# The last norm of a transformer trunk, moved from a stage of its own into the expert loop

## The chip, the cores and the metric

The kernel runs on one core of a Trainium2 chip. The metric is the device time of one execution in microseconds (us). Engines are named as in the profile: PE is TensorE, PEld its weight loads, DVE is VectorE, ACT is ScalarE, POOL is GpSimd, SP is SyncE (here it only issues DMAs). All data is float32.

## The reference, cut to what matters

One layer of a trunk over 2048 tokens of width 1024: token mixing, cross-attention to a memory, then a mixture of 32 experts, and a norm over the result. The change touches only the last two:

```python
def rmsnorm(x, g):
    y = x * rsqrt(mean(x * x, axis=-1) + EPS)
    return y * g

# group top-1, then the top 2 of its 8 experts: every token visits two experts
x = x + sum over the token's two experts e of gate * ((silu(h @ w1[e]) * (h @ w3[e])) @ w2[e])
return rmsnorm(x, norm_final)
```

## The kernel before, in words

The visits (two for each token, 4096 in all) are sorted by expert and padded to blocks of 128 slots for each expert. 47 blocks are in use in this run. route (from line 1849) works out for every slot its token (slot_rows, a row number; an empty slot has a number past the end, 4096, and an indirect DMA skips it) and its gate (slot_gates). hm_scratch holds the normed inputs of all tokens, x_scratch (x2 in the code) the residual stream in DRAM.

run_experts (line 2051) goes through the blocks, one "turn" for each. Each engine has its own written-out order, and they meet at semaphores:

- TensorE, step(b): the products with w1 and w3 into g_ps and u_ps, the transposes of the next block's inputs (xg), the product with w2 of the block before into y_ps, the transposes of h. Each product is made of three, of parts cut high and low (split_product).
- ScalarE, step(b): cuts the high parts of the next expert's w13 weights (high_w13, line 1830), silu, the high part of x, then scales y_ps by the gates into exp_y (line 2215), which waits for y_free, then the high part of h and of w2 (line 2224).
- DVE, step(b): the low parts of the same (lines 1834, 2262, 2238, 2258), 12 operations of 128x1024 in a block that is the first of its expert, and silu times u.
- POOL, in a turn: gather(b + 3) brings the inputs of a later block from hm_scratch into xg (line 1845), after TensorE's transposes of the block before it; scatter(b) waits that the scatter before has landed, raises y_free, waits for ScalarE's scaling (y_scaled), copies the slot's rows (line 2156) and adds exp_y to x_scratch by an indirect DMA with an add (line 2159).
- SP loads the weights: next_w13 for expert e when the products of expert e - 2 are done, next_w2 likewise.

When the last scatter has landed, POOL raises all_stored, and SP loads the first tiles of x_scratch and the gains over the weights (FinishLoads). finish_norm (line 2326) then runs over 16 tiles of 128 tokens: load (SP), square with a sum (ScalarE, line 2362), mean (DVE, line 2374), power of -1/2 (POOL, line 2350), scaling by that and by the gains (DVE, line 2378), store (ScalarE's queue).

## Time and profile before

| | us |
|---|---|
| median of 3 runs | 2643.79 (2642.81 to 2645.5) |
| the profiled execution | 2644.87 |
| its span in the trace | 2643.1 |
| TensorE busy | 2515.5 (95%) |
| DVE, ScalarE, POOL busy | 1477.4, 1284.2, 603.5 |
| last scatter starts | 2590.84 |

Times in the rows are us from the start of the span, unless marked ns. A group of instructions shows how many there were (x47), their busy time, the mean ns of one, and what the engine had waited for ahead of them. POOL's DMA_INDIRECT is the generation of descriptors; the transfer itself goes on after it, up to its landing.

### The profile page before, as it was taken

To read this page: it belongs to the slowest core of one execution; us is meant where nothing else is said; L and a number is where in the kernel's file an instruction comes from. 1 tells how busy PE (TensorE), PEld (TensorE's weight loads), DVE (VectorE), ACT (ScalarE), POOL (GpSimd) and SP (SyncE) were. 2 spreads that over 40 slices of the span, in tenths; PEclk is the share of its full clock that TensorE was granted. 3 is DMA by queue.
4 is the path that set the end of the run, shared out by engine and by line. 5 is a ranking of instruction groups with operands and counts; after the bars stand their busy time and mean duration, and the time that the engine had idled before them with its cause. 6 is when DMAs were issued, how large, how long until landed. Compare 5 with 4: busy or idle time off the path is not lost. (4 is left out here: it accounts for less than half of the span.)

```text
span 2643.1 us, 44806 instructions
## 1 busy us (share of the span) xinstructions
PE 2515.5 (95%) x14538; PEld 2053.4 (78%) x14539; DVE 1477.4 (56%) x1943; ACT 1284.2 (49%) x2286; POOL 603.5 (23%) x650
## 2 busy tenths in 40 slices
PE   9999999999999999989999999799999999999991
PEld 7888888676666678886888888678877888888880
DVE  5221343698888864444333333666988755565653
ACT  5221211698898941133222222346878654565643
POOL 0000011477777720000000000012212222112223
PEclk9999999999999999999999999799999999999996
DMA  7433231314201033233121221448999866586757
GB/s 264 165 124 125 84 150 42 100 34 148 73 18 45 2 120 120 96 148 108 62 89 71 92 74 66 170 147 303 388 376 372 295 208 202 197 293 209 264 162 273
DMA packets 141439, 414.83 MB, mean 157 GB/s; under 512 B 22016, under 2 KB 30720, under 8 KB 140288
## 3 DMA queue, kind: packets, MB, share of 16 engines
q1 hardware_dynamic: 125040, 371.15, 38.0%
q0 software_dynamic: 13968, 33.59, 5.4%
q10 hardware_dynamic: 2304, 8.39, 0.8%
q8 instruction: 81, 1.33, 0.2%
q14 instruction: 46, 0.38, 0.0%
HBM read 338.60 MB, written 91.75 MB: 163 GB/s over the span
## 5 line engine op out<-in xcount | busy, mean ns | idle before, releaser
L685 POOL TENSOR_TENSOR stick_weight<-stick_weight,stick_left 128x512 f32<-128x512 f32 (+3 forms) x320 | 327.9, 1038 | 126.5 <-DVE stick_left L817 121.9
L1834 DVE TENSOR_TENSOR moe_w_lo<-moe_w_lo_raw,moe_w_hi (+1 forms) x256 | 298.6, 1219 | 61.9 <-ACT moe_w_hi L1830 32.2
L1830 ACT CAST moe_w_hi<-moe_w_lo_raw (+1 forms) x256 | 256.3, 1053 | 51.5 <-DMA moe_w_lo_raw<-in_w 25.6
L817 DVE TENSOR_TENSOR_SCAN stick_left<-stick_z_ps,stick_left,stick_any_row 128x512 f32<-128x512 f32 x192 | 240.1, 1274 | 35.4 <-ACT stick_z_ps L780 35.1
L778 ACT ACTIVATE stick_weight<-stick_z_ps 128x512 f32<-128x512 f32 (+3 forms) x320 | 173.7, 543 | 32.7 <-PE stick_z_ps L727 21.0
L740 PE MATMUL stick_t_ps<-all_ident,stick_weight 128*128 128x128 f32 x1088 | 165.3, 281 | 18.9 <-ACT stick_weight_t L787 9.1
L780 ACT ACTIVATE stick_z_ps<-stick_z_ps 128x512 f32<-128x512 f32 (+3 forms) x320 | 165.7, 518 | 10.2
L740 PEld LDWEIGHTS stick_t_ps<-all_ident,stick_weight 128*128 128x128 f32 x1088 | 116.0, 141 | 69.8 <-issue 46.1
L75 PE MATMUL exp_g_ps<-moe_w_hi,exp_x_hi 128*128 x376 | 151.8, 404 | 11.5 <-DVE exp_x_lo L2238 11.5
L1845 POOL DMA_INDIRECT moe_xg<-hm_scratch,moe_now x50 | 68.0, 1361 | 405.1 <-PE exp_x_ps L2274 268.0
L75 PE MATMUL proj_z_ps<-proj_w_hi,proj_h_hi 128*128 128x512 f32 x384 | 152.1, 396 | 2.5 <-DVE proj_h_lo L403 2.5
L2262 DVE TENSOR_TENSOR moe_w_lo<-moe_w_lo_raw,moe_w_hi 128x1024 f32 (+1 forms) x128 | 148.1, 1216 | 8.7 <-ACT moe_w_hi L2224 8.3
L75 PE MATMUL exp_y_ps<-moe_w_hi,exp_h_hi 128*128 128x512 f32 x376 | 150.4, 400 | 2.3 <-DVE exp_h_lo L2258 2.3
L76 PE MATMUL proj_z_ps<-proj_w_lo,proj_h_hi 128*128 128x512 f32 x384 | 150.2, 391 | 0.0
L77 PE MATMUL proj_z_ps<-proj_w_hi,proj_h_lo 128*128 128x512 f32 x384 | 150.1, 391 | 0.0
L77 PE MATMUL exp_g_ps<-moe_w_hi,exp_x_lo 128*128 x376 | 147.5, 392 | 0.0
L76 PE MATMUL exp_g_ps<-moe_w_lo,exp_x_hi 128*128 x376 | 147.0, 391 | 0.0
L77 PE MATMUL exp_y_ps<-moe_w_hi,exp_h_lo 128*128 128x512 f32 x376 | 147.0, 391 | 0.0
L76 PE MATMUL exp_y_ps<-moe_w_lo,exp_h_hi 128*128 x376 | 146.7, 390 | 0.0
L77 PE MATMUL exp_u_ps<-moe_w_hi,exp_x_lo 128*128 x376 | 146.6, 390 | 0.0
L75 PE MATMUL exp_u_ps<-moe_w_hi,exp_x_hi 128*128 x376 | 146.3, 389 | 0.0
L76 PE MATMUL exp_u_ps<-moe_w_lo,exp_x_hi 128*128 x376 | 146.3, 389 | 0.0
(291 smaller groups left out, 5811.4 us busy)
## 6 DMA issues: line engine op xcount, KB each, us to landing
moe_w_lo_raw<-in_w SPq DMA_DIRECT2D x384, 512.0 KB, 12.3
proj_w_lo_raw<-in_w_in SPq DMA_DIRECT2D x40, 256.0 KB, 6.3
proj_xs<-in_x SPq DMA_DIRECT2D x16, 512.0 KB, 4.5
qt_scratch<-proj_qk_out SPq DMA_DIRECT2D x16, 512.0 KB, 2.8
kt_scratch<-proj_qk_out SPq DMA_DIRECT2D x16, 512.0 KB, 2.7
mix_q<-qt_scratch SPq DMA_DIRECT2D x16, 512.0 KB
mix_out_xs<-in_x SPq DMA_DIRECT2D x16, 512.0 KB, 4.4
x_scratch<-mix_out_xs SPq DMA_DIRECT2D x16, 512.0 KB, 3.0
```

The source lines that it names most:

```text
L75: pe.matmul(out, left_hi, right_hi, start=first, stop=False)
L76: pe.matmul(out, left_hi, right_lo, start=False, stop=False)
L77: return pe.matmul(out, left_lo, right_hi, start=False, stop=last)
L685: nc.gpsimd.tensor_tensor(taken, taken, after, ALU.mult).then_inc(weight_done, 1)
L740: last = nc.tensor.transpose(t_ps[:, n % 2, b], weight[:, n % W_SLOTS, b * P:(b + 1) * P], ident)
L778: nc.scalar.activation(weight[:, n % W_SLOTS, 0:keys], z, ACT.Sigmoid).then_inc(take_done, 1)
L780: nc.scalar.activation(z, z, ACT.Sigmoid, scale=-1.0).then_inc(leave_done, 1)
L817: nc.vector.tensor_tensor_scan(row[:, c * BANK:c * BANK + keys][:, ::-1], back, any_row[:, 0:keys], start, ALU.mult, ALU.bypass).then_inc( ...
L1830: nc.scalar.copy(self.w13_hi[:, self.w13_at(e, i)], self.w13_raw[:, self.w13_at(e, i)]).then_inc(self.w13_cut, 1)
L1834: ops.tensor_tensor(self.w13_lo[:, self.w13_at(e, i)], self.w13_raw[:, self.w13_at(e, i)], as_f32(self.w13_hi[:, self.w13_at(e, i)]), ALU. ...
L1845: nc.gpsimd.indirect_dma_start(out=self.xg[:], out_offset=None, in_=self.hm, in_offset=bass.IndirectOffsetOnAxis(ap=self.now[:].bitcast(U3 ...
L2262: nc.vector.tensor_tensor(w2_lo[:, w2_at(e, i)], w2_raw[:, w2_at(e, i)], as_f32(w2_hi[:, i]), ALU.subtract).then_inc(w2_ready, 1)
```

## The change

There is no last stage. A token's last visit is the one in the later block. route marks it (is_last) and adds 2048 to the row number of that slot. So slot_rows tells three kinds of slots apart: below 2048 (first visit), 2048 to 4095 (last visit), 4096 (empty).

- scatter(b) adds exp_y to x_scratch for first visits only; the others are out of bounds and skipped.
- ask(b) brings the residual rows of a block's last visits from x_scratch into a new tile end_sb; it is issued at the end of the turn before. list_ends makes the row numbers for it in four small operations.
- finish(b) adds exp_y to end_sb on POOL, ScalarE squares end_sb with a sum, POOL multiplies end_sb by the gains into exp_y once the scatter has landed, makes mean plus EPS and its power, scales exp_y by it, and writes exp_y to the output rows by an indirect DMA. y_free is raised when that DMA (out_stored) has landed. A row whose sum is not complete or a slot that is empty is skipped.
- gather makes its row numbers with two more small operations.
- The silu is written into exp_h instead of a tile of its own, to make room; DVE multiplies in place. ScalarE's silu then waits for the transposes of h. The square's unused output lies over exp_h.
- The gains are loaded by SP within the expert loop, and POOL waits for them ahead of scatter(0).
- FinishLoads and finish_norm are gone.

```diff
     def gather(self, nc, pool, b, slot_rows, xt_done):
         wait_past(pool, self.gathered, 16 * b)
-        nc.gpsimd.tensor_copy(self.now[:], slot_rows[:, bass.ds(b, 1)]).then_inc(self.listed, 1)
+        tokens = self.hm.shape[0]
+        nc.gpsimd.tensor_copy(self.now[:, 7:8], slot_rows[:, bass.ds(b, 1)]).then_inc(self.copied, 1)
+        pool.wait_ge(self.copied, b + 1)
+        pool.sem_inc(self.list_seen, 1)
+        nc.gpsimd.tensor_scalar(self.now[:, 4:5], self.now[:, 7:8], tokens, tokens, ALU.is_ge, ALU.mult).then_inc(self.halved, 1)
+        pool.wait_ge(self.halved, b + 1)
+        pool.sem_inc(self.list_seen, 1)
+        nc.gpsimd.tensor_tensor(self.now[:, 0:1], self.now[:, 7:8], self.now[:, 4:5], ALU.subtract).then_inc(self.listed, 1)
...
+                for k in range(2):
+                    link(nc.vector.tensor_tensor(is_last[:, k], dest[:, k], dest[:, 1 - k], ALU.is_gt))
+                link(nc.vector.scalar_tensor_tensor(out=token_end[:], in0=is_last[:], scalar=float(tiles * P),
+                                                    in1=token[:].unsqueeze(1).broadcast_to([P, 2, tiles]), op0=ALU.mult, op1=ALU.add))
...
                 next_w2(1, True)
+                sp.dma_start(gains[:], gain_out.partition_broadcast(P)).then_inc(gains_loaded, 16)
                 with sp.Fori(3, experts) as e:
                     next_w13(e)
                     next_w2(e - 1, False)
                 next_w2(experts - 1, False)
-                sp.wait_ge(all_stored, 1)
...
                 def scatter(b):
                     if not isinstance(b, int):
-                        pool.wait_ge(stored, 16 * b)
+                        pool.wait_ge(out_stored, 16 * b)
                         pool.sem_inc(y_free, 1)
                     pool.wait_ge(y_scaled, b + LEAD + 1)
...
+                def finish(b):
+                    if isinstance(b, int):
+                        pool.wait_ge(end_cleared, 1)
+                        list_ends(b)
+                        pool.wait_ge(ask_listed, 1)
+                    else:
+                        pool.wait_ge(asked, 16 * b)
+                    nc.gpsimd.tensor_tensor(end_sb[:], end_sb[:], y_sb[:], ALU.add).then_inc(added, 1)
+                    nc.gpsimd.tensor_copy(end_now, ask_now).then_inc(end_listed, 1)
+                    pool.wait_ge(added, b + 1)
+                    pool.sem_inc(end_seen, 1)
+                    pool.wait_ge(stored, 16 * (b + 1))
+                    nc.gpsimd.tensor_tensor(y_sb[:], end_sb[:], gains[:], ALU.mult).then_inc(weighed, 1)
+                    pool.wait_ge(squared, b + LEAD + 1)
+                    pool.sem_inc(end_seen, 1)
+                    nc.gpsimd.tensor_scalar(half[:, 2:3], half[:, 1:2], EPS, None, ALU.add).then_inc(meaned, 1)
+                    pool.wait_ge(meaned, b + 1)
+                    nc.gpsimd.tensor_tensor(half[:, 3:4], half[:, 2:3], half[:, 0:1], ALU.pow).then_inc(rooted, 1)
+                    pool.wait_ge(rooted, b + 1)
+                    pool.wait_ge(weighed, b + 1)
+                    pool.sem_inc(end_seen, 1)
+                    nc.gpsimd.tensor_scalar(y_sb[:], y_sb[:], half[:, 3:4], None, ALU.mult).then_inc(ended, 1)
+                    pool.wait_ge(ended, b + 1)
+                    pool.wait_ge(end_listed, b + 1)
+                    pool.sem_inc(end_seen, 1)
+                    nc.gpsimd.indirect_dma_start(out=out, out_offset=bass.IndirectOffsetOnAxis(ap=end_now.bitcast(U32), axis=0),
+                                                 in_=y_sb[:], in_offset=None,
+                                                 bounds_check=tokens - 1, oob_is_err=False).then_inc(out_stored, 16)
+
+                def list_ends(b):
+                    nc.gpsimd.tensor_copy(store.now[:, 7:8], slot_rows[:, bass.ds(b, 1)]).then_inc(row_copied, 1)
...
+                    nc.gpsimd.tensor_scalar(is_more, store.now[:, 7:8], tokens, 3 * tokens, ALU.is_lt, ALU.mult).then_inc(more_marked, 1)
...
+                    nc.gpsimd.tensor_scalar(add_now, is_more, -tokens, None, ALU.add).then_inc(add_marked, 1)
...
+                    nc.gpsimd.tensor_tensor(ask_now, store.now[:, 7:8], add_now, ALU.add).then_inc(ask_listed, 1)
+
+                def ask(b):
+                    list_ends(b)
+                    pool.wait_ge(ask_listed, b + 1)
+                    pool.sem_inc(ask_seen, 1)
+                    nc.gpsimd.indirect_dma_start(out=end_sb[:], out_offset=None, in_=x2,
+                                                 in_offset=bass.IndirectOffsetOnAxis(ap=ask_now.bitcast(U32), axis=0),
+                                                 bounds_check=tokens - 1, oob_is_err=False).then_inc(asked, 16)
...
+                pool.wait_ge(gains_loaded, 16)
                 scatter(0)
+                finish(0)
+                ask(1)
                 with pool.Fori(1, used) as b:
                     gather(b + 3)
                     scatter(b)
+                    finish(b)
+                    ask(b + 1)
...
                         act.wait_ge(g_done, b + 1)
                         if not first:
-                            act.wait_ge(gated, b)
-                        nc.scalar.activation(g_sb[:], g_ps[:], ACT.Silu).then_inc(silu_done, 1)
+                            act.wait_ge(ht_done, b)
+                            act.wait_ge(squared, b)
+                        nc.scalar.activation(h_sb[:], g_ps[:], ACT.Silu).then_inc(silu_done, 1)
...
+                    if not first:
+                        act.wait_ge(added, b)
+                        nc.scalar.activation(junk[:], end_sb[:], ACT.Square, scale=width ** -0.5, accum_out=half[:, 1:2]).then_inc(squared, 1)
...
-                        if not first:
-                            dve.wait_ge(ht_done, b)
-                        nc.vector.tensor_tensor(h_sb[:], u_ps[:], g_sb[:], ALU.mult).then_inc(gated, 1)
+                        nc.vector.tensor_tensor(h_sb[:], u_ps[:], h_sb[:], ALU.mult).then_inc(gated, 1)
```

## Rows read from the trace of the kernel before

**Rows 1.** The page's busy times of each engine over the span.

```profile
PE 2515.5 (95%) x14538; PEld 2053.4 (78%) x14539; DVE 1477.4 (56%) x1943; ACT 1284.2 (49%) x2286; POOL 603.5 (23%) x650
```

**Rows 2.** Windows, by stretch: stretch, length, busy us per engine, PEclk, DMA share, GB/s.

```profile
1907.32:2077.91 170.59, 162.23 (x757) 132.85 (x756) 147.62 (x145) 136.01 (x164) 37.34 (x36) 1.00 1.00 374
2077.91:2574.89 496.98, 496.51 (x2353) 414.41 (x2352) 282.33 (x294) 266.65 (x350) 104.14 (x112) 1.00 0.65 222
```

**Rows 3.** Timeline of ScalarE: start us, duration, what, [idle before].

```profile
1770.19 1.27 ACT L2215 ACTIVATE exp_y<-exp_y_ps,all_slot_gates 128x512 f32<-128x512 f32 x2 [4.52 <-PE exp_y_ps L77]
...
2579.52 1.26 ACT L2215 ACTIVATE exp_y<-exp_y_ps,all_slot_gates 128x512 f32<-128x512 f32 x2 [4.50 <-PE exp_y_ps L77]
...
2588.32 1.26 ACT L2215 ACTIVATE exp_y<-exp_y_ps,all_slot_gates 128x512 f32<-128x512 f32 x2 [7.06 <-POOLq L2154]
```

**Rows 4.** The chain of waits that ended last, its last piece.

```profile
2636.00 1.28 DVE all_end_xs L2378
```

**Rows 5.** Timeline of POOL: the first scatter, then one late turn.

```profile
1772.65 1.63 POOL L2159 DMA_INDIRECT x_scratch<-exp_y,exp_rows_now  x1 [0.95 <-POOL exp_rows_now L2156]
...
2574.89 1.06 POOL L1845 DMA_INDIRECT moe_xg<-hm_scratch,moe_now  x1 [7.97 <-PE exp_x_ps L2274]
...
2582.04 1.61 POOL L2159 DMA_INDIRECT x_scratch<-exp_y,exp_rows_now  x1 [0.92 <-POOL exp_rows_now L2156]
```

**Rows 6.** The scatter's source line, and the DMA view behind two scatters (1808.13, 2192.14).

```profile
DMA to landing us min/median/max: 4.5/9.1/10.6
...
q0 software_dynamic: 148, 0.52, 22.1%
x_scratch<-exp_y,exp_rows_now POOLq DMA_INDIRECT x1, 10.4
...
q0 software_dynamic: 144, 0.12, 7.4%
x_scratch<-exp_y,exp_rows_now POOLq DMA_INDIRECT x1, 4.5
```

**Rows 7.** Timeline of POOL: an early gather, and the copy that waits for its landing.

```profile
1749.53 1.02 POOL L1845 DMA_INDIRECT moe_xg<-hm_scratch,moe_now  x1 [12.48 <-issue]
1753.83 0.91 POOL L1840 COPY moe_now<-all_slot_rows 128x1 int32<-128x1 int32 x1 [3.29 <-DMA moe_xg<-hm_scratch,moe_now]
```

**Rows 8.** Groups and source lines: prices of POOL operations, and the square on ScalarE.

```profile
L685 POOL TENSOR_TENSOR stick_weight<-stick_weight,stick_left x320: 403/1092/1290, 487.0 to 938.2; 128x512 f32<-128x512 f32 x112, 128x128 f32<-128x128 f32 x16, 128x256 f32<-128x256 f32 x16, 128x384 f32<-128x384 f32 x16
...
L294 POOL TENSOR_TENSOR proj_stat<-proj_stat,all_half 128x1 f32<-128x1 f32 x16 | 8.8, 548 | 171.1 <-DVE proj_stat L394 171.1
L1980 POOL MEMSET moe_xg<- 128x1024 f32 x1 | 1.0, 951 | 9.8 <-POOLq L33 9.8
L290 POOL TENSOR_SCALAR_AFFINE_SELECT all_ident<-all_ident 128x128 f32<-128x128 f32 x1 | 0.3, 284 | 0.2 <-POOL mix_above L287 0.2
...
L2362 ACT ACTIVATE end_junk<-all_end_xs 128x1024 bf16<-128x1024 f32 x16 | 16.9, 1057 | 26.2 <-DMA all_end_xs<-x_scratch 12.2 <-PEq L33 11.9 <-DVE all_end_xs L2378 1.8
```

**Rows 9.** DVE's cuts and POOL's index copy as groups; then POOL beside DVE, timeline.

```profile
L1834 DVE TENSOR_TENSOR moe_w_lo<-moe_w_lo_raw,moe_w_hi (+1 forms) x256 | 298.6, 1219 | 61.9 <-ACT moe_w_hi L1830 32.2
...
L2156 POOL COPY exp_rows_now<-all_slot_rows x47: 181/181/1176, 1771.5 to 2589.7; 128x1 int32 x46, 128x1 int32<-128x1 int32 x1
...
2082.76 2.35 DVE L1834 TENSOR_TENSOR moe_w_lo<-moe_w_lo_raw,moe_w_hi  x2
...
2083.97 1.18 POOL L2156 COPY exp_rows_now<-all_slot_rows 128x1 int32 x1 [4.56 <-ACT exp_y L2215]
...
2629.25 1.28 DVE L2378 SCALAR_TENSOR_TENSOR all_end_xs<-all_end_xs,end_stat,all_end_gains 128x1024 f32<-128x1024 f32 x1
2629.41 1.52 POOL L2350 TENSOR_TENSOR end_stat<-end_stat,all_half 128x1 f32<-128x1 f32 x1 [0.97 <-DVE end_stat L2374]
```

**Rows 10.** SP's timeline of weight loads; then the windows view behind them.

```profile
1769.08 2.33 SPq L1825 DMA_DIRECT2D moe_w_lo_raw<-in_w  x4
...
1787.00:1791.00 4.00, 4.00 (x21) 3.32 (x20) 0.90 (x2) 3.09 (x5) 0.74 (x2) 1.00 0.04 17
```

More of the change, by code:

```diff
@@ L1805, in __init__ @@
         self.w2_lo, self.w2_raw = s.two_views("w2_lo", [P, 2 * self.w2_size])
-        self.now = s.sbuf("now", [P, 1], I32)
         self.xg = s.sbuf("xg", [P, self.width])
+        self.now_at = s.next_at() + 4 * (2 * self.rows * P + self.hidden + 2 * self.h_rows * P + 2 * self.width)
+        self.now = s.over("now", [P, 8], I32, self.now_at)
         self.w13_loaded = [s.sem(f"w13_loaded{i}") for i in range(self.rows)]
@@ L2025, in _, with run_experts @@
                                      in_block[:, c % DEPTH, at].rearrange("p k b -> p (k b)"), start=n == 0, stop=n == pairs - 1).then_inc(slotted, 1)
[L2028 to L2051 removed]
+def run_experts(nc, store, gain_out, gains, slot_rows, slot_gates, block_end, block_expert, block_kind, n_blocks, ident, half, x2, out):
     experts, width, hidden = store.w1.shape
@@ L2066, in run_experts @@
     with ExitStack() as stack:
-        s = Scope(nc, stack, "exp")
-        rows_now = s.sbuf("rows_now", [P, 1], I32)
+        s = Scope(nc, stack, "exp", store.at % LINE)
+        more_now, ask_now, end_now = (store.now[:, i:i + 1] for i in range(1, 4))
+        is_more, add_now = (store.now[:, i:i + 1] for i in range(5, 7))
         x_hi, x_lo = s.sbuf("x_hi", [P, rows, P], F32R), s.sbuf("x_lo", [P, rows, P], F32R)
-        g_sb = s.sbuf("g", [P, hidden])
+        h_at = s.next_at()
         h_sb = s.sbuf("h", [P, hidden])
+        junk = s.over("junk", [P, width], BF16, h_at)
+        assert 2 * width <= 4 * hidden
         h_hi, h_lo = s.sbuf("h_hi", [P, h_rows, P], F32R), s.sbuf("h_lo", [P, h_rows, P], F32R)
         y_sb = s.sbuf("y", [P, width])
+        end_sb = s.sbuf("end", [P, width])
+        assert s.next_at() == store.now_at
         x_ps = s.psum("x_ps", [P, rows, P])
@@ L2139, in _ @@
                 next_w2(experts - 1, False)
-                sp.wait_ge(all_stored, 1)
-                for n in range(finish.GROUP):
-                    finish.load_x(sp, n)
-                    if n == 0:
-                        finish.load_gains(sp)
             @block.gpsimd
@@ L2170, in _ @@
                     scatter(b)
+                    finish(b)
+                    ask(b + 1)
                 pool.wait_ge(gathered, 16 * used + 48)
-                pool.wait_ge(stored, 16 * used)
-                pool.sem_inc(all_stored, 1)
+                pool.wait_ge(asked, 16 * used)
+                pool.wait_ge(out_stored, 16 * used)
             @block.scalar
@@ L2178, in _ @@
                 act.sem_inc(y_scaled, LEAD)
+                act.sem_inc(squared, LEAD)
                 def cut_w13(e, these):
```

110 lines of the change are left out of this document (27 added, 83 removed).

## The prediction

> **What bounds the kernel now.** The page's busy times come first: TensorE is busy 95% of the span [rows 1], so a change pays only where TensorE idles or is made to idle. The busy times by stretch show two stages of the expert loop, one with the transfers saturated and one with TensorE alone full; TensorE is idle 8.4 us of 170.6 in the first and 0.5 us of 497.0 in the second [rows 2]. ScalarE's timeline gives the pace of the loop: the first scaling of a block's output starts at 1770.19 and the 47th at 2588.32 [rows 3], so 46 turns take 818.1 us, 17.8 us each. The chain of waits shows the end: after the last scaling the last scatter lands, then loads, norms and stores follow, and the last stage's last scaling begins only at 2636.00 [rows 4]. From 2588.3 to the end of the span (2643.1) TensorE does nothing: 54.8 us, what the change can win. The price is on POOL, whose timeline [rows 5] has one scatter and one gather in a turn, with long pauses.
>
> **What is removed.** The 16 loads and stores, squarings and scalings of the last stage go. What remains behind the last exp_y scaling is one turn's chain: by the items below the output DMA starts 2.5 + 5.4 + 2.0 + 1.2 + 1.2 + 0.9 = 13.2 us on, the last request for residual rows 1.6 + 1.4 + 0.9 later, and it lands after 4.3: 21.4, say 22 us. So the end gives 54.8 - 22 = 33 us.
>
> **What is added: one serial loop.** The output buffer exp_y is single. Before, it came free when the scatter had landed. Now POOL keeps it until the norm is written into it and the output rows have landed, and the wait for that (in scatter) stands behind this turn's request for residual rows and the next turn's gather in POOL's order. So the next scaling on ScalarE waits for nearly everything that POOL does in a turn; that is the loop whose length I sum. The gather's wait for TensorE's transposes is over by then, since TensorE needs 17.8 us for its own turn.
>
> 1. Scaling start to scatter start: 2579.52 to 2582.04 [rows 3, 5], 2.5 us.
> 2. Landing of the scatter, which the multiplication by the gains waits for, as it overwrites exp_y. It was 4.5/9.1/10.6 us; 0.12 MB took 4.5 and 0.52 MB took 10.4 [rows 6]. Half of all visits are last ones and leave this scatter. The two cases give 14.8 us per MB, and an average scatter (4096 visits of 4 KB over 47 blocks, 0.36 MB) loses half: 0.18 MB, an estimated 5.4 us. It now starts 4 us behind a gather, which needs 4.3 us (1749.53 to 1753.83 [rows 7]), where there were 7, so I take 6.5; the ends are 4.5 and 9.1. The addition, its index copy and ScalarE's square are hidden here: scatter 1.6, addition 2.0, square 1.1 [rows 5, 8] are 4.7 us. With the cover gone they would cost the difference.
> 3. Multiplication 128x1024 on POOL. Only 128x128 (0.40 us) and 128x512 (1.09) are in the trace [rows 8]; the slope gives 2.0 us (ends 0.95, the 128x1024 memset, and 2.4, the longest 128x512, 1.29, doubled less one start).
> 4. Mean, power, and its semaphores: the power alone is 0.55 us, a dependent start 0.2 [rows 8], a small copy 0.18 [rows 9]: 1.2 us.
> 5. Scaling by a column, 128x1024, one input: between the memset of 0.95 and the two-input 2.0 [rows 8]; nearer the memset, 1.2.
> 6. Output DMA: 0.9 us from its index to its start and 1.6 us of generating [rows 5]: 2.5.
> 7. Four small operations of list_ends, each 0.18 and a gap of about 0.2: 1.4; the request 0.9 + 1.0 [rows 5, 7]: 3.3 together.
> 8. The next gather, three small ones at 0.35 and 0.9 + 1.0: 3.0.
> 9. The output rows have landed by then (6 us after their start, as in 2); the semaphore and ScalarE's start, 0.2.
>
> Sum: 2.5 + 6.5 + 2.0 + 1.2 + 1.2 + 2.5 + 3.3 + 3.0 + 0.2 = 22.4 us. Even at every lower end (landing 4.5, multiplication and scaling 0.95) it is 19.1, over the 17.8 of now.
>
> **DVE beside it.** A POOL operation that starts beside a long DVE operation reading two tensors in SBUF ends only after it: the 0.18 us copy took 1.18 at 2083.97 and the 0.55 us power 1.52 at 2629.41, each up to the end of DVE's [rows 9], about 0.95 more each. DVE's cuts of weights are such operations, 12 in each of 31 blocks that cut the next expert's weights (256 of w13 less the first 8, by 8 [rows 9]), 14.6 us at 1.22. In a turn of some 28 us half of it is covered by them; of POOL's 13 operations behind the landing half meet one: 13 x 0.5 x 0.95 = 6.2 us. Ends: nothing, and 13 x 0.95 = 12.4. So 28.6 us in 31 turns and 22.4 in 15: mean 26.6.
>
> The Trainium skill (DMA: Bandwidth & Descriptors, section "Anatomy of one DMA — SWDGE (gpsimd) path") speaks for a cheaper landing: 2.0 us and the bytes at 436 GB/s, by which 0.18 MB would land in 2.4 us as an estimate and the sum would be 46 x 3 = 138 us smaller than with my 5.4. The trace disagrees: no scatter landed below 4.5 us [rows 6].
>
> **Other edits.** scatter(0) now waits for the gains, whose load stands on SP's queue behind weight loads, the last of them issued at 1771.4 [rows 10]. The transfers are idle from 1787 on [rows 10], so the gains land near 1787 and the first scatter (1772.65 before [rows 5]) slips 14 us; between 0, if it were absorbed, and 18, the end of that idle window. It lies on the serial loop, so nothing takes it back. ScalarE's new wait for the addition stands ahead of the next block's weight cuts: the addition ends 2.5 + 1.6 + 2.0 = 6.1 us behind the scaling, when ScalarE has just done its w2 cuts, and the square is 1.1 us more; what queues behind it (cuts, then silu, then TensorE's next products) has the 9 us by which the loop outlasts TensorE's turn. The silu into exp_h waits for transposes that are long done: nothing. Routing gets three small DVE operations, 0.5 us. The transfers: half the scatter's bytes go, as many are read and as many written in the loop, 0.5 MB less over a longer turn than the loop moves already; DMA share is 0.65 in most of it [rows 2], so nothing.
>
> **The sum.** 46 turns x 26.6 = 1223.6 against 818.1: +405. End -33, gains +14, routing +0.5: +386. The profiled execution took 2644.87 us for a span of 2643.1, 1.1 us over the median of the runs, 2643.79. So 2643.8 + 386 = 3030 us.
>
> **Rivals.**
> - B, **DVE costs POOL nothing**: the cuts and POOL's operations fall apart in time, since the longer turn leaves DVE idle half of it. For it: the copy before the scatter was mostly undisturbed, its median 0.18 [rows 9]. Against it: the held copy and power [rows 9]. All turns 22.4: 46 x 4.6 = +212, less 18.5: 2837 us. Chance 0.24.
> - C, **landing and port both at the bad end**: the scatter still lands in 9.1 us [rows 6] (behind the gather, beside weight loads), and 10 of the 13 operations meet a cut: turns of 25.0 and 34.5 us, mean 31.4, +626 - 18: 3251 us. Chance 0.13. The Trainium skill (SBUF — State Buffer, section "Who interferes with whom") says that whoever comes second on this pair of ports blocks for the whole instruction, DVE too; no row here shows DVE held, and by it POOL's three wide operations, an estimated 5 us a turn, would delay the weight cuts.
> - D, **the loop fits under TensorE**: faster. The place is the wait for out_stored ahead of y_free in scatter; if POOL's turn were at most 17.8 us, it would cost nothing, and the result would be 2643.8 - 33 = 2611, with the gains' slip caught up in POOL's pauses. It decides from 17.8 us; at 18.2 us a turn the win of the end is used up. For it: POOL is busy only 23% of the span. Against it: the lower ends sum to 19.1, so it needs transfers that land in about 2.5 us. Chance 0.04.
> - E, about as before, with a turn near 18.2 us. Chance 0.01.
> - The forecast A, 0.58.
>
> **How the numbers follow.** The predicted time is A's, 3030. Its own range comes from its terms: landing 4.5 to 9.1 is -2.0 to +2.6 us a turn, the wait for DVE 6.2 +- 3 in two thirds of the turns; -3 to +3.5 a turn is about 2890 to 3190. The range of 8 in 10 reaches down to B and keeps out C's upper part, D and E: 2810 to 3200. A measurement of this kernel can tell 0.2% (5.3 us) from no change. Faster 0.04, within 0.2% 0.01, slower 0.95.
>
> **What would show it.** In the profile after, the start of one scaling of exp_y to the next should be 22 to 29 us, released by POOL at the wait in scatter, longer in blocks with weight cuts. TensorE should idle some 9 us in each turn, just ahead of the exp_y products, and its granted clock may sag there. POOL's small copies beside cuts should take about 1.1 us, those apart 0.2. The first scatter should start near 1787, and 20 to 25 us should lie between the last scaling and the end. It is wrong if the scalings stay 18 us apart, or if ScalarE waits for the addition rather than for the buffer.

## The result and the profile after

| | before | after |
|---|---|---|
| median of 4 runs each, us | 2644.64 (2642.81 to 2648.44) | 3004.93 (3001.42 to 3006.95) |
| after over before, 95% interval | | 1.1356 (1.1342 to 1.1369) |
| predicted, range | | 3030, 2810 to 3200 |
| span of the profiled execution, us | 2643.1 | 3005.1 |

The changed kernel is 13.6% slower: +360.3 us, where +386 were forecast. The page of the kernel after, its busy times and its row of granted clocks; they answer to [rows 1].

```profile
PE 2642.8 (88%) x14538; PEld 2133.8 (71%) x14539; DVE 1650.1 (55%) x1914; ACT 1312.6 (44%) x2348; POOL 1328.9 (44%) x1303
PEclk9999999999999999999999898888888888888887
```

POOL's busy time has more than doubled (603.5 to 1328.9 us). TensorE has the same 14538 matmuls and is busy 127 us longer, at a lower granted clock in the stretch of the experts. ScalarE's timeline gives the pace, as in [rows 3]:

```profile
1770.59 1.27 ACT L2270 ACTIVATE exp_y<-exp_y_ps,all_slot_gates 128x512 f32<-128x512 f32 x2 [4.52 <-PE exp_y_ps L77]
...
2401.81 1.27 ACT L2270 ACTIVATE exp_y<-exp_y_ps,all_slot_gates 128x512 f32<-128x512 f32 x2 [10.20 <-POOLq L2149]
...
2983.11 1.27 ACT L2270 ACTIVATE exp_y<-exp_y_ps,all_slot_gates 128x512 f32<-128x512 f32 x2 [13.12 <-POOLq L2149]
```

The first scaling starts within 0.4 us of its old place, so all that stands ahead of the experts is unchanged. The 47th starts at 2983.11 instead of 2588.32: 46 turns take 1212.5 us, 26.4 each, against 17.8. The 17.8 are a mean of 45 turns of 18.0 and a last one of 8.8 (2579.52 to 2588.32 in [rows 3]), which has no next block to work on; the last turn is now 22.0, nearly as long as the others. From it to the end of the span lie 22.0 us instead of 54.8. The windows view of the loop and of the end, columns as in [rows 2]:

```profile
1770.59:2983.11 1212.52, 934.31 (x3807) 750.19 (x3805) 730.51 (x545) 548.10 (x730) 904.93 (x832) 0.86 0.55 190
2983.11:3005.10 21.99, 0.00 (x0) 0.00 (x0) 0.00 (x0) 2.41 (x4) 14.54 (x15) 0.50 0.04 14
```

POOL has 904.9 us of work in the 1212.5, 19.7 in each turn; before there were 3.9. The rest of a turn is starts of DMAs and semaphores between its own instructions. The waits of that stretch, with their sum, count and longest:

```profile
ACT exp_y L2270 <- POOLq L2149: 481.1, 45, 16.4
PE exp_y_ps L75 <- DVE moe_w_lo L2318: 144.6, 30, 6.7
ACT exp_junk L2282 <- POOL exp_end L2166: 124.4, 46, 19.5
...
PE exp_h_ps L2375 <- DVE exp_h L2308: 93.7, 29, 15.6
```

The scaling waits 10.7 us in 45 of the 46 turns for the signal that POOL gives (L2149). Three further waits stand beside it: TensorE for DVE's w2 cuts, which were no wait before, ScalarE's square for POOL's addition, and TensorE's transposes of h for the product that DVE makes behind the later silu. POOL's costliest groups of that stretch:

```profile
L2180 POOL TENSOR_SCALAR exp_y<-exp_y,all_half 128x1024 f32<-128x1024 f32 x46 | 176.8, 3844 | 11.2 <-POOL all_half L2176 11.2
L2166 POOL TENSOR_TENSOR exp_end<-exp_end,exp_y 128x1024 f32<-128x1024 f32 x46 | 135.7, 2950 | 0.2 <-DMA exp_end<-x_scratch,moe_now 0.2
L2171 POOL TENSOR_TENSOR exp_y<-exp_end,pre_end_gains 128x1024 f32<-128x1024 f32 x46 | 126.2, 2743 | 27.5 <-DMA x_scratch<-exp_y,moe_now 27.2
...
L2176 POOL TENSOR_TENSOR all_half<-all_half 128x1 f32<-128x1 f32 x46 | 61.4, 1334 | 3.8
...
L2174 POOL TENSOR_SCALAR all_half<-all_half 128x1 f32<-128x1 f32 x46 | 46.3, 1006 | 3.9
```

The scaling by the root's column is the dearest, 3.84 us. Mean and power together take 2.34 instead of some 0.8. The gain product waits for the scatter only 27.2 us in all, in 23 of the 46 turns.

**One turn without a weight cut.** It is the last, 2961.14 to 2983.11, in POOL's timeline:

```profile
2964.77 1.63 POOL L2154 DMA_INDIRECT x_scratch<-exp_y,moe_now  x1 [2.02 <-issue]
2965.88 2.92 POOL L2166 TENSOR_TENSOR exp_end<-exp_end,exp_y 128x1024 f32<-128x1024 f32 x1
...
2969.05 2.39 POOL L2171 TENSOR_TENSOR exp_y<-exp_end,pre_end_gains 128x1024 f32<-128x1024 f32 x1
...
2972.67 2.87 POOL L2180 TENSOR_SCALAR exp_y<-exp_y,all_half 128x1024 f32<-128x1024 f32 x1 [0.24 <-POOL all_half L2176]
...
2976.47 1.11 POOL L2184 DMA_INDIRECT out_x<-exp_y,moe_now  x1 [0.94 <-POOL exp_y L2180]
...
2979.97 1.14 POOL L2206 DMA_INDIRECT exp_end<-x_scratch,moe_now  x1 [0.93 <-POOL moe_now L2199]
...
2983.05 1.12 POOL L1853 DMA_INDIRECT moe_xg<-hm_scratch,moe_now  x1 [0.91 <-issue]
```

Nothing waits here for a landing: from the scatter at 2964.77 on POOL goes from one instruction to the next, with its starts of 0.9 us between them.

**The same stretch beside four w2 cuts**, timelines of DVE, POOL and TensorE from 2404:

```profile
2404.71 10.47 DVE L2318 TENSOR_TENSOR moe_w_lo<-moe_w_lo_raw,moe_w_hi 128x1024 f32 x4 [0.43 <-ACT moe_w_hi L2279]
...
2405.44 2.96 POOL L2166 TENSOR_TENSOR exp_end<-exp_end,exp_y 128x1024 f32<-128x1024 f32 x1
...
2408.94 2.87 POOL L2171 TENSOR_TENSOR exp_y<-exp_end,pre_end_gains 128x1024 f32<-128x1024 f32 x1
2411.89 1.10 POOL L2174 TENSOR_SCALAR all_half<-all_half 128x1 f32<-128x1 f32 x1
2413.08 1.40 POOL L2176 TENSOR_TENSOR all_half<-all_half 128x1 f32<-128x1 f32 x1
...
2415.23 0.80 PE L75 MATMUL exp_y_ps<-moe_w_hi,exp_h_hi 128*128 128x512 f32 x1 [6.39 <-DVE moe_w_lo L2318]
```

Both sides lose. Four cuts take 10.47 us where four at 1.22 are 4.9. The mean takes 1.10 instead of 0.24 and the power 1.40 instead of 0.58 in the free turn. TensorE waits 6.39 us for the cuts, but its products were still done long before ScalarE could use them: the next scaling, at 2425.74, waited for POOL. Over the stretch, the two groups of cuts in DVE's table, and then the w2 cuts of the kernel before in the same stretch:

```profile
L2318 DVE TENSOR_TENSOR moe_w_lo<-moe_w_lo_raw,moe_w_hi 128x1024 f32 (+1 forms) x124 | 311.8, 2573 | 12.9 <-ACT moe_w_hi L2279 12.9
L1835 DVE TENSOR_TENSOR moe_w_lo<-moe_w_lo_raw,moe_w_hi x240 | 309.3, 1347 | 125.4 <-ACT moe_w_hi L1831 125.4
```

```profile
L2262 DVE TENSOR_TENSOR moe_w_lo<-moe_w_lo_raw,moe_w_hi 128x1024 f32 (+1 forms) x124 | 143.5, 1216 | 8.7 <-ACT moe_w_hi L2224 8.3 <-issue 0.4
```

The w2 cuts, which meet POOL's wide operations, are doubled to 2.57 us; the w13 cuts, later in the turn, grow by a tenth. The scatter's own landing (its source line; [rows 6] had 4.5/9.1/10.6):

```profile
DMA to landing us min/median/max: 2.8/4.8/6.6
```

### The profile page after: what moved, and what is told of

It is laid out like the page before. It is cut to its first block and busy times, and to the rows that moved or that the text cites. A ratio compares the mean times of both kernels' runs of the same rounds, so it can differ in the third digit from the quotient of the medians.

```text
span 3005.1 us, 46073 instructions
## 1 busy us (share of the span) xinstructions
PE 2642.8 (88%) x14538; PEld 2133.8 (71%) x14539; DVE 1650.1 (55%) x1914; ACT 1312.6 (44%) x2348; POOL 1328.9 (44%) x1303
## 3 DMA queue, kind: packets, MB, share of 16 engines
q8 instruction: 81, 1.33, 0.2%
## 5 line engine op out<-in xcount | busy, mean ns | idle before, releaser
L1835 DVE TENSOR_TENSOR moe_w_lo<-moe_w_lo_raw,moe_w_hi (+1 forms) x256 | 327.9, 1339 | 131.5 <-ACT moe_w_hi L1831 129.3
L2318 DVE TENSOR_TENSOR moe_w_lo<-moe_w_lo_raw,moe_w_hi 128x1024 f32 (+1 forms) x128 | 316.5, 2530 | 12.9 <-ACT moe_w_hi L2279 12.9
L75 PE MATMUL exp_y_ps<-moe_w_hi,exp_h_hi 128*128 128x512 f32 x376 | 178.5, 475 | 152.1 <-DVE moe_w_lo L2318 144.6
L2270 ACT ACTIVATE exp_y<-exp_y_ps,all_slot_gates 128x512 f32<-128x512 f32 x94 | 59.5, 684 | 501.4 <-POOLq L2149 481.1
L1831 ACT CAST moe_w_hi<-moe_w_lo_raw (+1 forms) x256 | 252.5, 1047 | 36.3 <-issue 23.9
L2314 DVE TENSOR_TENSOR exp_h_lo<-exp_h_ps,exp_h_hi 128x512 fp32r<-128x512 f32 x47 | 32.5, 692 | 327.4 <-ACT exp_h_hi L2275 327.4
L75 PEld LDWEIGHTS exp_y_ps<-moe_w_hi,exp_h_hi 128*128 128x128 f32 x376 | 85.8, 228 | 176.7 <-DVE moe_w_lo L2318 150.3
L75 PE MATMUL exp_g_ps<-moe_w_hi,exp_x_hi 128*128 x376 | 169.5, 451 | 23.4 <-DVE exp_x_lo L2296 23.4
L2180 POOL TENSOR_SCALAR exp_y<-exp_y,all_half 128x1024 f32<-128x1024 f32 x47 | 179.7, 3823 | 11.4 <-POOL all_half L2176 11.4
L76 PE MATMUL exp_y_ps<-moe_w_lo,exp_h_hi 128*128 x376 | 170.1, 452 | 0.0
L77 PE MATMUL exp_y_ps<-moe_w_hi,exp_h_lo 128*128 128x512 f32 x376 | 167.7, 446 | 0.0
```

Source lines behind the costliest of these rows:

```text
L75: pe.matmul(out, left_hi, right_hi, start=first, stop=False)
L76: pe.matmul(out, left_hi, right_lo, start=False, stop=False)
L77: return pe.matmul(out, left_lo, right_hi, start=False, stop=last)
L1831: nc.scalar.copy(self.w13_hi[:, self.w13_at(e, i)], self.w13_raw[:, self.w13_at(e, i)]).then_inc(self.w13_cut, 1)
L1835: ops.tensor_tensor(self.w13_lo[:, self.w13_at(e, i)], self.w13_raw[:, self.w13_at(e, i)], as_f32(self.w13_hi[:, self.w13_at(e, i)]), ALU. ...
L2180: nc.gpsimd.tensor_scalar(y_sb[:], y_sb[:], half[:, 3:4], None, ALU.mult).then_inc(ended, 1)
```

## Experiments

All times stand against runs of the kernel before on the same chip (2644.1 to 2646.7 us). The prices of a turn are read from the first to the 47th scaling.

**The gains loaded first.** Their load goes ahead of the weight loads behind which it stood.

```diff
+                sp.dma_start(gains[:], gain_out.partition_broadcast(P)).then_inc(gains_loaded, 16)
                 next_w13(2)
                 next_w2(1, True)
-                sp.dma_start(gains[:], gain_out.partition_broadcast(P)).then_inc(gains_loaded, 16)
```

> The changed kernel with one edit: the gains are loaded ahead of the weight loads in the expert loop. A (POOL's loop over the one output buffer is serial, so a late start of its first turn is never caught up): the time from the first to the second scaling of exp_y falls from 38.5 us to the 24.7 of the next one, and the whole from 3004.9 to 2991. Rival (a late first turn is absorbed by pauses): the first turn shortens, the rest gives it back, 3005.

Measured 2998.37 us (4 runs, ratio 1.134, 1.1321 to 1.1359); 6.6 less than the changed kernel. POOL's timeline of this kernel:

```profile
1773.98 1.64 POOL L2154 DMA_INDIRECT x_scratch<-exp_y,moe_now  x1 [0.95 <-POOL moe_now L2151]
...
1784.18 2.50 POOL L2171 TENSOR_TENSOR exp_y<-exp_end,pre_end_gains 128x1024 f32<-128x1024 f32 x1 [4.52 <-DMA x_scratch<-exp_y,moe_now]
```

The first scatter starts at 1773.98 instead of 1786.25. But now its landing takes some 10 us, beside the weight loads that the gains had let pass. The first turn is 30.8 us instead of 38.5, so 7.7 of the 13.8 us of slip come back, and the other turns keep their pace (25.99 us against 26.09). The runs of the two kernels nearly touch (2995.8 to 3002.0 against 3001.4 to 3007.0), so the evidence is the first turn and not the total. The slip is not absorbed, as the rival had it, but A took the landing for unchanged and had twice the gain.

**No scaling by the column.** Leaves out L2180: the output rows are not divided by their norm.

```diff
                     pool.sem_inc(end_seen, 1)
-                    nc.gpsimd.tensor_scalar(y_sb[:], y_sb[:], half[:, 3:4], None, ALU.mult).then_inc(ended, 1)
-                    pool.wait_ge(ended, b + 1)
```

> The changed kernel without POOL's scaling of exp_y by the column of roots; the rows written are not divided by their norm. A (the turn is the sum of POOL's chain): every turn loses the operation's mean 3.8 us and its 0.2 us start, 46 turns and the end: 3004.9 - 47 x 4.0 = 2817, turns of 22.1 us. Rival (landing of transfers, or TensorE's wait for DVE's w2 cuts, 144.6 us in all, sets the turn beside POOL): turns shrink by a third of that at most, 2940 or more.

Measured 2889.77 us (1 run): -115, where theory A had -188 and the rival at most -65. A turn falls from 26.36 to 23.85, by 2.5 of the 4 us taken out. The two groups that took the rest back, in this kernel:

```profile
L2171 POOL TENSOR_TENSOR exp_y<-exp_end,pre_end_gains 128x1024 f32<-128x1024 f32 x46 | 132.2, 2874 | 46.9 <-DMA x_scratch<-exp_y,moe_now 46.7
...
L2182 POOL DMA_INDIRECT out_x<-exp_y,moe_now x46 | 71.2, 1548 | 47.7 <-issue 47.7
```

The wait for the scatter grows from 27.2 to 46.7 us, and the output DMA (1.31 before) and the index operations behind it move up beside DVE's cuts and are held in the scaling's place. So POOL's work is on the path, but a microsecond of this operation is worth some 0.6.

**One-input cuts on DVE.** The low parts of w13, and in the same way those of w2, are the raw weights times a constant instead of the remainder of the cut; the number and size of the cuts stay.

```diff
-        ops.tensor_tensor(self.w13_lo[:, self.w13_at(e, i)], self.w13_raw[:, self.w13_at(e, i)],
-                          as_f32(self.w13_hi[:, self.w13_at(e, i)]), ALU.subtract).then_inc(self.w13_ready, 1)
+        ops.tensor_scalar(self.w13_lo[:, self.w13_at(e, i)], self.w13_raw[:, self.w13_at(e, i)],
+                          2.0 ** -12, None, ALU.mult).then_inc(self.w13_ready, 1)
...
```

> The changed kernel with DVE's 12 low cuts of a turn made operations of one input (the loaded weights times 2^-12 instead of loaded less high; the low parts are wrong values, the rest is the same). A (DVE's two-input operations hold POOL's, and are held by them): POOL's addition falls from 2.95 us towards 2.34, small operations no longer take 1.0, turns with cuts come down to the 24 us of those without, 31 x 3 less: 2912. Rival (turns with cuts are longer for their transfers and ScalarE's order): the turns stay at 27 and the time at 3005.

Measured 2948.03 us (1 run): -57. Groups of this kernel:

```profile
L2180 POOL TENSOR_SCALAR exp_y<-exp_y,all_half 128x1024 f32<-128x1024 f32 x46 | 151.6, 3295 | 11.2 <-POOL all_half L2176 11.2
...
L2318 DVE TENSOR_SCALAR moe_w_lo<-moe_w_lo_raw (+1 forms) x124 | 223.7, 1860 | 13.9 <-ACT moe_w_hi L2279 13.9
L1835 DVE TENSOR_SCALAR moe_w_lo<-moe_w_lo_raw x240 | 201.7, 874 | 159.8 <-ACT moe_w_hi L1831 158.9
```

Between the two expectations. The holding lessens (column scaling 3.84 to 3.30, power 1.33 to 1.01) and does not end. DVE's one-input cut takes 0.87 us in the mean late in the turn (0.69 in the median) and 1.86 beside POOL's wide operations. The Trainium skill (SBUF — State Buffer, section "Who interferes with whom") says that a one-input DVE operation stays clear of GpSimd unless it runs in a mode that uses both port pairs; the 0.69 us against 1.22 for two inputs agree with such a mode, though no row names it. The gain lies in one part of the loop. The 31 turns behind 2190 fall from 25.6 to 23.9 us. The 12 turns ahead of them, from 1861 on, where weights are loaded all the time, fall only from 27.3 to 26.9, for there POOL's wait for the scatter's landing grows from 5.4 to 37.9 us. The edit makes the cuts shorter as well as one-input, and no measured run has none. So this run shows that DVE's cuts lengthen the turn, and not which of the two counts, or what a turn without any holding would cost.

**Prices of POOL operations by themselves.** Five operations on a cleared tile while the tokens are routed, with only small pieces on DVE beside them.

```diff
+                nc.gpsimd.tensor_tensor(xv, xv, xv, ALU.mult).then_inc(store.xg_cleared, 1)
...
+                nc.gpsimd.tensor_scalar(xv, xv, 0.5, None, ALU.mult).then_inc(store.xg_cleared, 1)
...
+                nc.gpsimd.tensor_scalar(xv, xv, col, None, ALU.mult).then_inc(store.xg_cleared, 1)
...
+                nc.gpsimd.tensor_tensor(xv, xv, col.broadcast_to([P, store.width]), ALU.mult).then_inc(store.xg_cleared, 1)
...
+                nc.gpsimd.tensor_scalar(store.xg[:, 0:512], store.xg[:, 0:512], col, None, ALU.mult).then_inc(store.xg_cleared, 1)
...
```

> The changed kernel, with five more POOL operations on the cleared input tile while routing runs on DVE, to price them away from the loop: a product of two 128x1024 inputs, a scaling by a constant, a scaling by a column, a product with that column broadcast, and a scaling by a column of 128x512. A (a scaling by a column costs POOL more than a second full input, whatever DVE does): 2.3, 1.1 to 2.3, 4.2, 2.3 and 2.1 us. Rival (the 3.8 us mean in the loop is DVE's hold on a 1.2 us operation): 2.3, 1.1, 1.2, 2.3, 0.7. The total stays at 3005, since POOL is idle there.

Measured 3012.78 us (1 run). POOL's timeline of this kernel:

```profile
1695.72 1.90 POOL L1998 TENSOR_TENSOR moe_xg<-moe_xg 128x1024 f32<-128x1024 f32 x1
1697.71 2.82 POOL L2000 TENSOR_SCALAR moe_xg<-moe_xg 128x1024 f32<-128x1024 f32 x1
1700.63 2.85 POOL L2002 TENSOR_SCALAR moe_xg<-moe_xg,pre_lane 128x1024 f32<-128x1024 f32 x1
1703.56 1.89 POOL L2004 TENSOR_TENSOR moe_xg<-moe_xg,pre_lane 128x1024 f32<-128x1024 f32 x1
1705.56 1.57 POOL L2006 TENSOR_SCALAR moe_xg<-moe_xg,pre_lane 128x512 f32<-128x512 f32 x1
```

Neither expectation: the one-input scaling costs 2.85 us by itself, more than a two-input product (1.90), and by a constant as much as by a column. That product reads one tile twice; the product of two tiles took 2.39 us in the turn without a cut, where the scaling took 2.87. The scaling is slow as an instruction, and another 1.0 us of its 3.84 in the loop is holding. The total was expected to stay at 3005 and is 8 us longer. The first scaling comes 4.4 us later here, and DVE's small steps of routing stand longer beside these operations: one on 128x4 that starts at 1695.89 takes 1.75 us and ends with POOL's product.

**The column broadcast in a two-input product** in place of L2180's form.

```diff
-                    nc.gpsimd.tensor_scalar(y_sb[:], y_sb[:], half[:, 3:4], None, ALU.mult).then_inc(ended, 1)
+                    nc.gpsimd.tensor_tensor(y_sb[:], y_sb[:], half[:, 3:4].broadcast_to([P, width]), ALU.mult).then_inc(ended, 1)
```

> One instruction of the changed kernel is exchanged: POOL's scaling of the 128x1024 rows by the root's column, a one-input form, becomes a two-input product with that column broadcast. In the routing stretch, with nothing beside it, the first took 2.85 us and the second 1.90; in the loop the first takes 3.82 on average over full and cut turns, the two-input add 2.95 and the product with the gains 2.73. Theory A, the form sets the price and VectorE's cuts hold both alike: the group falls from 3.82 to about 2.8, by 1.0 us a turn. When the scaling was left out, 62 of each 100 ns saved came back in the turn (2.5 of 4.0 us), so 47 turns give back 30 to 48 us: 2957 to 2975, point 2968. Rival, a one-input scaling is slow because it is held, and a two-input form beside VectorE's two-input cuts is held more: the group stays at 3.6 or more and the time at 2995 to 3010.

Measured 2962.01 us (4 runs, ratio 1.1206, 1.1188 to 1.1225): -43, theory A. Its group in POOL's table:

```profile
L2180 POOL TENSOR_TENSOR exp_y<-exp_y,all_half 128x1024 f32<-128x1024 f32 x47 | 103.0, 2192 | 9.9 <-POOL all_half L2176 9.9
```

3.82 to 2.19 us: 1.6 a turn, where A had 1.0, of which the turns (25.37) give back 1.0. The share of 0.6 holds again.

**Norm on DVE.** One DVE instruction takes the place of POOL's product and scaling.

```diff
-                    nc.gpsimd.tensor_tensor(y_sb[:], end_sb[:], gains[:], ALU.mult).then_inc(weighed, 1)
...
-                    nc.gpsimd.tensor_scalar(y_sb[:], y_sb[:], half[:, 3:4], None, ALU.mult).then_inc(ended, 1)
...
+                        dve.wait_ge(rooted, b)
+                        nc.vector.scalar_tensor_tensor(out=y_sb[:], in0=end_sb[:], scalar=half[:, 3:4], in1=gains[:],
+                                                       op0=ALU.mult, op1=ALU.mult).then_inc(ended, 1)
```

> The changed kernel with the multiplication by the gains and the scaling by the roots as one DVE operation at the end of its step, in place of POOL's two. A (sum of POOL's chain): a turn loses 2.7 + 3.8 + 0.4 us and gains 1.3 + 0.2: 5.4 less, 20.7 us a turn, 3004.9 - 47 x 5.4 = 2751. Rival (DVE's order takes the place: the operation stands behind four w2 cuts, which POOL's addition holds up): 24 us in turns with cuts, 20.7 in the others, 2850.

Measured 2846.66 us (4 runs, ratio 1.076, 1.0742 to 1.0778): -158, 22.96 a turn, where A had 2751 and the rival 2850. The waits that took the rest:

```profile
POOL out_x L2179 <- DVE exp_y L2316: 104.6, 46, 2.8
POOL all_half L2173 <- DMA x_scratch<-exp_y,moe_now: 99.9, 31, 6.1
```

6.6 us of POOL's work went out of a turn and the turn fell by 3.4. Against it stand POOL's new wait for DVE's product (104.6 us, 2.3 a turn), which is the rival's, and the longer one for the scatter's landing (99.9 instead of 27.2 us, 1.6 a turn more), which nothing covers now. Together they are 3.9 and more than the missing 3.2, as some of what is left is held less (the power takes 0.62 us instead of 1.33).

**The output released by its landing.** ScalarE waits for the landing of the output rows itself, not for POOL's signal behind request and gather.

```diff
-                        act.wait_ge(y_free, b)
+                        act.wait_ge(out_stored, 16 * b)
```

> The changed kernel with one way of releasing altered: ScalarE's scaling waits for the landing of the output rows itself instead of for the signal that POOL gives behind its request and its next gather. In the last turn of the changed kernel the output DMA starts at 2976.47 and the signal comes 6.6 us later; a landing of 4.5 to 5.5 us would let the scaling start 1 to 2 us earlier. Theory A, it is POOL's own work that fills the turn, not the buffer: POOL is idle between its gather and its index copy for the scatter only 0.4 us, and that is all there is to win: 46 turns by 0.4 are 17 us, 2988, range 2980 to 2997. Rival, the buffer's loop is what is closed and everything behind the scaling moves up with it: 46 turns by 1 to 2 us are 46 to 92 us, 2913 to 2959.

Measured 3004.79 us (4 runs, 2994.92 to 3014.38; ratio 1.1342, 1.1321 to 1.1362): nothing, neither the rival's 2913 to 2959 nor A's 2988. The first scaling comes 20.8 us later here, as it waits for an added first output DMA behind the gains, but the second only 2.8 us later, so the pace is read from there on: 26.1 us a turn in both kernels. ScalarE's wait in this kernel, and then the gain product in POOL's table:

```profile
ACT exp_y L2274 <- DMA out_x<-exp_y,moe_now: 344.0, 45, 13.6
```

```profile
L2168 POOL TENSOR_TENSOR exp_y<-exp_end,pre_end_gains 128x1024 f32<-128x1024 f32 x46 | 118.1, 2568 | 59.3 <-DMA x_scratch<-exp_y,moe_now 58.3
```

The rival is out: the release no longer stands behind POOL's request and gather, and the mean turn stays. Single turns do not: they now take 20 to 34 us where they took 22 to 29. Even A's 0.4 us a turn went; POOL's wait for the scatter grew beside it (27.2 to 58.3 us). What closes the loop is what POOL does in its order, landing of the scatter included, and not the signal.

**Rows read back.** Another way to have no last stage: the scatter adds all visits as before, and a turn later the rows that are final are read back, squared on ScalarE, scaled on DVE in place and stored. The output buffer is free when the scatter has landed; POOL has no wide operation. This kernel and the two after it also load the gains first.

```diff
-                    nc.gpsimd.tensor_tensor(end_sb[:], end_sb[:], y_sb[:], ALU.add).then_inc(added, 1)
...
+                    pool.wait_ge(stored, 16 * b)
+                    pool.sem_inc(y_free, 1)
+                    pool.wait_ge(out_stored, 16 * b)
+                    ask(b - 1, b + 1)
                     scatter(b)
+                    root(b + 1)
+                    send(b + 1)
```

> The norm stays in the expert loop but off the output buffer: all visits are added to x_scratch by the scatter as before the change, exp_y comes free when that has landed, and only then, one turn later, the finished rows of last visits are read back into end_sb, squared by ScalarE between its w2 casts, scaled in place by one DVE operation, and written. A (what costs is POOL's chain inside the loop over exp_y; taken off it, the turn is TensorE's again): turns of 17.8 us, 19 to 20 in the stretch with saturated transfers, 24 us from the last scaling to the end: 2620 to 2635, faster than both. Rival 1 (DVE, 16.4 us busy in turns with cuts and 1.3 more here, becomes the bound, and POOL waits for it): those turns 19.5, 2670. Rival 2 (POOL's order itself, five operations with transfers and their small copies, passes 18 us): turns of 21, 2780.

Measured 2730.18 us (4 runs, ratio 1.032, 1.0302 to 1.0337): A's 2620 to 2635 is out, and the time lies between the rivals' 2670 and 2780. Its DVE cuts are back at 1.22 us. Turns are 22 to 25.6 us from 1845 to 2175, where weights for each block are loaded (17.7 to 19.0 before). Of the 32 others most take 17.7 to 19.5, against 17.7 before, and seven take 20 to 22.4. ScalarE's timeline in that stretch:

```profile
2116.32 1.06 ACT L2274 ACTIVATE exp_junk<-exp_end 128x1024 bf16<-128x1024 f32 x1 [6.11 <-DMA exp_end<-x_scratch,moe_now]
```

The square stands amid the w2 cuts and waits for a read that was issued at 2108.92, while weights are loaded: 163.1 us in 37 turns. That this wait makes those turns long is argued; the next run moves the square, and the time does not fall.

**Read back, squared later.** The square goes behind four w13 cuts of the next turn and DVE's product behind six.

```diff
                         cut_w13(e + 1, range(0, 4))
+                    if not first:
+                        act.wait_ge(ht_done, b)
+                        square(b)
```

> The kernel that scatters every visit and reads the rows back a turn later, with ScalarE's square moved from amid its w2 cuts to behind the w13 cuts of the next turn, and VectorE's product likewise, so that neither queue stands at a read that has not landed. Theory A, the 163 us in which ScalarE waited for the read's landing were what made the turns of the stretch full of weight loads 22 to 25.6 us: they fall to about 20, the turns of the other stretches stay at 17.7 to 19, the end takes 30 to 35 us. 2730 less 163 times a half to two thirds (a part of the waiting stood beside weights that had not come either) gives 2620 to 2660, point 2655. Rival, the one buffer that request, square, product and output take in turn is a chain of its own, two landings of up to 7 us each and about 7 us of work, and it is longer than a turn in that stretch: the turns there stay at 22 or more, the wait moves to POOL's request <- landing of the output, and the time is 2700 to 2730.

Measured 2776.17 us (4 runs, ratio 1.049, 1.0472 to 1.0507): slower than the kernel it was to mend, beyond both theories. The waits of its loop:

```profile
ACT exp_y L2260 <- POOLq L2202: 187.7, 34, 7.3
POOL out_x L2181 <- DVE exp_end L2321: 179.1, 47, 6.2
```

POOL stands at the output rows for DVE's later product, and the signal that frees the output buffer comes behind them. From 2162 on turns of 16 to 17 us mostly alternate with turns of 22 to 26.

**That signal taken out of POOL's order.** ScalarE waits for the scatter's landing itself.

```diff
-                        act.wait_ge(y_free, b)
+                        act.wait_ge(stored, 16 * b)
```

> The kernel before this one with one way of releasing changed: ScalarE's scaling waits for the landing of the scatter by itself instead of for a signal that POOL gives behind its output rows and its next gather. Theory A, the signal made the turns of 24 to 26 us that alternate with 16 to 17 us where no weights are late, and the 188 us that the scaling waited: without it the 30 turns outside the saturated stretch fall from 20.4 on average to about 17.9, and in that stretch the chain of the one buffer (request, square, product, output, 22.5 us closed in the trace) loses at best 1.5 of its 22.5 us. 2776 less 30 times 2.5 is 2701, less 16 times 0 to 1.5 is 2677 to 2701: point 2690. Rival, the chain of the one buffer and not the signal is what holds the turns outside that stretch too, ScalarE then standing at the square for the read's landing: the time stays at 2755 to 2780.

Measured 2767.95 us (4 runs, ratio 1.0464, 1.0447 to 1.0482), the rival's range. ScalarE's longest wait in the loop:

```profile
ACT exp_junk L2277 <- DMA exp_end<-x_scratch,moe_now: 281.8, 45, 18.9
```

The wait for the signal is gone and the wait for the read has grown from 141.6 to 281.8 us over the span. By the trace it is the one buffer of rows (request, square, product, output) that closes: in the loop POOL stands 185.2 us for DVE's product, and 64.9 us for the landing of the output rows ahead of the next request. Three requests in a row start at 2284.09, 2301.83 and 2324.84, 17.7 and 23.0 us apart, and the mean turn is 20.6. No run has a second such buffer, so what it would give is not shown. No version beats the kernel before.

## Why the prediction was right, and where its terms were not

The forecast was case A, one serial loop that POOL fills, some of it held by DVE. It is what happened: 46 turns of 26.36 us, the slip of the gains in them, against 26.6 without that slip and 26.9 with it, an end of 22.0 against 22, 360 us in all against 386. Its terms in the order of its list, the free turn (2961.14) and the mean of 46 turns beside them:

| step | predicted | free turn | mean |
|---|---|---|---|
| 1 scaling to scatter | 2.5 | 3.6 | 2.8 |
| 2 scatter to gain product | 6.5 | 4.3 | 5.3 |
| 3 gain product | 2.0 | 2.4 | 2.7 |
| 4 mean, power, starts | 1.2 | 1.2 | 2.8 |
| 5 column scaling | 1.2 | 2.9 | 3.8 |
| 6 output DMA | 2.5 | 2.0 | 2.2 |
| 7 list_ends, request | 3.3 | 3.5 | 4.4 |
| 8, 9 gather, release | 3.2 | 2.0 | 2.2 |
| sum | 22.4 | 22.0 | 26.4 |
| DVE's holding | 4.2 (mean of 46) | none | in the steps above |

- **Step 1** held: 2.5 us in most turns (2983.11 to 2985.63). In the first turn it holds the gains' slip and in the free one a start of 2.02 instead of 0.9.
- **Step 2** named the wrong releaser for half of the turns: the product waits for the landing in 23 of the 46, for 1.2 us each. The scatter's landing was forecast at 6.5 us and is 4.8 in the median: the 5.4 from the slope of the two cases was near, and the 1.1 added for standing close behind a gather was not seen, though the scatter starts 2.6 us behind the gather and not 4. In the other turns, as from 2964.77 to 2969.05, what fills the time is POOL's addition, 2.92 us instead of the 2.0 given to it, and its index copy. There the landing is hidden and the addition is not, the reverse of the forecast. The term is 2.2 us smaller in the free turn and 1.2 in the mean. The estimate of 2.4 us by the Trainium skill (DMA: Bandwidth & Descriptors, "Anatomy of one DMA — SWDGE (gpsimd) path") lies below the shortest landing of 47, 2.8 us.
- **Step 5** failed as a size: taken at 1.2 as "nearer the memset", measured 2.85 by itself and 3.84 in the loop. The step in the argument was that one input must be cheaper than two. On POOL it was dearer, and the memset, which reads nothing, was no neighbour. The upper end of 2.0 was too low too.
- **Steps 3, 4, 6, 7** held within 0.5 us in the free turn.
- **Step 8** counted the gather's own start and 1.05 us of generating. The signal is given as the gather is issued (2983.05, and the scaling at 2983.11), so that part lies beside the scaling.
- **DVE's holding**: 6.2 us in 31 turns was a mean of 4.2; the free turn and the mean of all differ by 4.4. The 4.4 have 0.3 of the gains' slip and 0.6 of waiting for the landing in them, and the free turn starts its scatter 1.1 us late; without these they are 4.6. The size was right and the place was wrong: turns without w13 cuts were taken as free, but 15 of the 16 have w2 cuts and are held too, while 13 of the 29 with w13 cuts have no w2 cut. The turns without w13 cuts take 24.4 us on average, those with them, the first left out, 27.0: the step between them is 2.6 us instead of 6.2. Of the wide operations the product is held by 0.35 us and the column scaling by 1.0.
- **"No row shows DVE held"** was true of the kernel before. After the change DVE's w2 cuts take 2.57 us. The Trainium skill (SBUF — State Buffer, section "Who interferes with whom") says that the shared ports are an exclusive lock, and that a DVE instruction with two SBUF inputs contends for them with a GpSimd instruction that reads SBUF; the 2.57 us against 1.22 agree. By the trace it cost little, though no run has only POOL held: TensorE idles 278 us of the loop, and its 144.6 us of waiting for the cuts lie under ScalarE's 481.1.
- **Gains**: the first turn is 38.5 us against 24.7 for the second, 13.8 where 14 were forecast; the first scatter starts at 1786.25 where "near 1787" was said. With the load moved, 7.7 of them come back.
- **The end** gave 32.8 us where 33 were forecast.
- **Rival B** (2837, no holding) is not what runs: the small operations took 1.0 and 1.3 us on average. **C** (3251) had the landing at 9.1; no landing exceeded 6.6. **D** (2611) needed a turn of 17.8; the shortest was 22.0, and even with the norm on DVE it is 22.96 on average.
- Of the signs named in advance, the release by POOL, the longer turns with cuts, the sagging clock, the small operations at 1.1 us and the tail were all seen. "22 to 29" holds for every turn but the first. TensorE idles 6.0 us a turn and not 9, as its matmuls take 2.8 us a turn longer at the lower clock; half of that idling (144.6 us) is ahead of the exp_y products, and a third (93.7) ahead of the transposes of h.

The errors cancel, and that is luck: in the free turn step 2 with -2.2, gather -1.2 and output -0.5 stand against column scaling +1.7, the late scatter +1.1, product +0.4 and request +0.2. What carried the result was the count of what POOL issues in a turn, not the price of any one of it.

## What to carry to other kernels

When a change puts work on an engine inside a loop, sum everything that engine issues in one turn, starts of DMAs included, and compare the sum with the turn: POOL's busy share of 23% before said little, the 22.4 us summed in advance, and the 19.7 us busy that were measured, against a turn of 17.8 said all. An end of 33 us is not worth a loop of 47 turns that grows by more than 0.7 us each. When a piece is taken out of such a loop, count on less than all of it: the three removals here gave back 0.6, 0.6 and 0.5 of what they took out, as what was behind moves up beside other work and waits there.

## What was not expected of the hardware

- POOL's scaling of 128x1024 f32 with one input, by a constant or by a column, takes 2.82 and 2.85 us; a product of the tile with itself, or with the column broadcast, takes 1.90, and one of two tiles 2.39 in the turn without a cut. The exchange alone was worth 43 us.
- DVE and POOL hold each other in both directions in this kernel: cuts of 1.22 us took 2.57 on average and up to 4.8, the 0.24 us mean plus EPS 1.0, the 0.58 us power 1.3.
- POOL's addition is shown from 1.11 us behind its scatter's start, while that DMA is still being generated (1.63 us), and takes 2.92 us where the product of the same shape takes 2.39. It ends 4.03 us behind the scatter's start, which is 1.63 and 2.40: the overlap in the trace wins nothing.
- An indirect DMA costs POOL 0.9 us of start and 1.1 to 1.6 us of generating in the mean of each of the four kinds: some 9 us of a turn, as much as the three wide operations together.
- TensorE's granted clock fell from 1.00 to 0.86 in the loop, in which it idles 278 us in pieces of several us. The 3807 matmuls shown in it are busy 934.3 us, where those of before, as many, were busy 806.5. By the trace it cost nothing here, as POOL sets the turn.
